# Mean squares per token from rows of x on ScalarE, and the norm factor spread by four products of 32 rows

## The chip, the cores and the metric

One core of a Trainium2 chip runs the kernel. The metric is the device time of one execution in microseconds. The time before is the median of three runs.

## What is computed

One inference layer of a hybrid decoder, for a prompt of 1024 tokens and 8 sequences of 4 new tokens: 1056 tokens of width 1024, all in f32. What matters here is the root mean square norm ahead of the combined projection:

```
y = x32 * lax.rsqrt(jnp.mean(x32 * x32, axis=-1, keepdims=True) + NORM_EPS)
h = y * norm_g
proj = jnp.einsum('btd,de->bte', h, w_in)        # 1024 -> 4608
qa, ka, va, ga, xb, gb, qc, kc, vc, gc = jnp.split(proj, SPLIT_IDX, axis=-1)
y = x + jnp.einsum('bte,ed->btd', mixed, w_out)  # mixed: retention, RG-LRU, window attention
```

The factor rsqrt(mean square + eps) is one number for each token. It commutes with the projection, so it can be applied to the projection's results.

## The kernel before

x lies transposed in memory (`x_T`): the 1024 features in 8 blocks of 128 partitions, the tokens along the free axis in three chunks of 352 (`xs`). Each f32 product is made of three passes over high and low parts (`h_hi`, `h_lo`, and `w_part` for the weights; lines 409 to 411). The 4608 output columns are 18 units of 256. Unit 0 comes first (`first_unit`). Units `qk`, `gB`, `xb`, `gC`, `gA` have 6 groups of 352 tokens; units `v`, `kvC` and `qC` have 9 groups with tokens on the partitions, 256 columns wide. A group is 24 products, in two halves; after half s of unit u every engine runs its `side(u, s)`, which places the smaller work by hand. Groups of units from 1 on use three banks of PSUM in turn (`proj_bank`), so group g waits until group g - 3 was read (`freed`). All engines run in program order; TensorE, ScalarE (`act`), VectorE (`dve`), GpSimd (`pool`) and SP, on whose queue nearly all transfers stand, meet by semaphores. Retention, RG-LRU, attention and at last the product with `w_out` follow, all interleaved with the projection's units on TensorE.

The norm's factor is made in units 1 and 2. ScalarE squares `xs` in six pieces of 4 x 352 columns (`x_square`, L820, at `SQUARE_AT` in unit 1), VectorE adds the eight feature blocks to one, `sqs` (`square_sum`, L1157 to L1163), and TensorE adds over the partitions with nine products against a column of ones at (1, 10) (`token_squares`, L451). VectorE divides and adds eps (`token_scale`), GpSimd takes the power -0.5 (L1638), so `rcol` has the factor with tokens on the partitions, nine columns. Where tokens lie along the free axis, the factor must stand in all partitions: VectorE multiplies nine identity tiles by `rcol` (`scale_diagonals`, L1180), TensorE multiplies ones (128 x 128) by each diagonal at (2, 3) (`spread_scale`, L461), and ScalarE copies the three banks to `rb` at (2, 4) (`spread_copy`, L827). ScalarE's evacuations of unit 2 use `rcol`; `rb` is read first by GpSimd and VectorE behind it.

The loads of weights (`load_w`, one unit of 1 MB into `raw`) wait until both engines have made the parts of the unit before.

Of the kernel before, what the change touches and what calls it, by code (L numbers as in the profile page):

```python
# [21 lines left out]
ALU = mybir.AluOpType  # L22
# [3 lines left out]
P = 128  # L26
# [75 lines left out]
def layer(nc, io):  # L102
    gammas = [float(1.0 - 2.0 ** (-5.0 - h)) for h in range(H)]
    with ExitStack() as ctx:
# [66 lines left out]
        with ExitStack() as r:  # L171

            sb("mixed_s", [P, 3 * H, TOK], scope=r)
            sb("under_v", [P, 2 * (NT + 1) * UNIT + N_CR], scope=r)
            sqt = sb("sqt", [P, 4 * CH], scope=r)
            sqs = sb("sqs", [P, TOK], scope=r)
            dgs = sb("dgs", [P, TOK], scope=r)
        with ExitStack() as r:
# [22 lines left out]
        with ExitStack() as r:  # L201
# [12 lines left out]

        names = """par_in ident_in const_in cr_in wg_in cc_in raw_in s0_in kcache_in vcache_in
            w0_in0 w0_in1 w0_in2 w0_in3 x_in0 x_in1 x_in2 x_in3 x_in4 x_in5 x_in6 x_in7 x_in8 x_in9 x_in10 x_in11
            x_again0 x_again1 x_again2 wo_in0 wo_in1 wo_in2 wo_in3
            stored_cache stored_ret stored_tails stored_kv stored_y0 stored_y1 stored_y2
            ones_set h_hi_set h_lo_set hs_set sq_set sq_added ms_done e9_set rcol_set ecol_set diag_set spread rb_set
            row_set gate_set ga_set ga_silu w_hi_set w_lo_set proj_done act_freed fold_set folded  # L220
# [22 lines left out]

        block = ctx.enter_context(nc.Block())

        def tile_rows(t):
# [12 lines left out]
        def _(sp):  # L259
# [26 lines left out]
            for c in range(1, 3):  # L286
# [3 lines left out]
            load_w(1)  # L290
            sp.dma_start(ident[:], io["c_ident"]).then_inc(S_["ident_in"], 16)
            sp.dma_start(gain[:].rearrange("p a d -> p (a d)"), io["qk_gain"].partition_broadcast(P)).then_inc(
                S_["const_in"], 16)
            sp.dma_start(st_T[:].rearrange("p f n -> p (f n)"), io["state_T"]).then_inc(S_["const_in"], 16)
            sp.dma_start(cr[:], io["c_ret"]).then_inc(S_["cr_in"], 16)

            for hd in range(H):
                if hd > 0:
                    sp.wait_ge(S_["stored_ret"], 32 * hd)
                else:  # L300
                    load_w(2)
                    load_w(3)
                    sp.wait_ge(S_["rb_set"], 3)
                sp.dma_start(s0[:], io["state_ret"][:, hd].rearrange("b d e -> d b e")).then_inc(S_["s0_in"], 16)
# [97 lines left out]
        WARM = 11  # L402
        SQUARE_AT = {0: (0, 0), 1: (0, 1), 2: (1, 0), 4: (1, 1), 6: (2, 0), 8: (2, 1)}

        @block.tensor
        def _(pe):
# [318 lines left out]
            def side(u, s):  # L725
                if u in RET_UNIT and s < 12:
# [7 lines left out]
                    if s < 9:  # L734
                        ret_one(base + s)
                if (u, s) == (1, 10):
                    token_squares()
                if (u, s) == (2, 3):
# [59 lines left out]
        def _(act):  # L798
# [17 lines left out]

            def x_square(c, half):
                if c + half > 0:
                    act.wait_ge(S_["sq_added"], 2 * c + half)
                act.activation(sqt[:].rearrange("p (k n) -> p k n", k=4), xs[c][:, 4 * half:4 * half + 4, :],  # L820
                               ACT.Square).then_inc(S_["sq_set"], 1)

            def spread_copy():
                for i in range(3):
                    n = 4 * P if i < 2 else NS
                    act.wait_ge(S_["spread"], i + 1)
                    act.activation(rb[:, i * 4 * P:i * 4 * P + n], bb[2 + i][:, 0:n], ACT.Copy).then_inc(  # L827
                        S_["rb_set"], 1)

# [301 lines left out]
        def _(dve):  # L1131
# [20 lines left out]

            def square_sum(c, half):

                total = sqs[:, c * CH:(c + 1) * CH]
                dve.wait_ge(S_["sq_set"], 2 * c + half + 1)
                link(dve.tensor_tensor(sqt[:, 0:2 * CH], sqt[:, 0:2 * CH], sqt[:, 2 * CH:4 * CH], ALU.add))  # L1157
                if half == 0:
                    dve.tensor_tensor(total, sqt[:, 0:CH], sqt[:, CH:2 * CH], ALU.add).then_inc(S_["sq_added"], 1)
                    return  # L1160
                link(dve.tensor_tensor(sqt[:, 0:CH], sqt[:, 0:CH], sqt[:, CH:2 * CH], ALU.add))
                dve.wait_ge(S_["sq_added"], 2 * c + 1)
                dve.tensor_tensor(total, total, sqt[:, 0:CH], ALU.add).then_inc(S_["sq_added"], 1)  # L1163

            def token_scale():

                link(dve.memset(ecol, 1.0))
                dve.wait_ge(S_["ms_done"], 1)
                pairs = bb[4][:, 0:2 * NT + 2].rearrange("p (t two) -> p t two", two=2)
                dve.tensor_scalar(ecol[:, 0:NT], pairs[:, 0:NT, 0], 1.0 / D, EPS, ALU.mult, ALU.add).then_inc(  # L1170
                    S_["e9_set"], 1)
                dve.tensor_scalar(ecol[0:NS, NT:NT + 1], pairs[0:NS, NT, 0:1], 1.0 / D, EPS, ALU.mult,
                                  ALU.add).then_inc(S_["e9_set"], 1)

            def scale_diagonals():
                dve.wait_ge(S_["ident_in"], 16)
                dve.wait_ge(S_["rcol_set"], 3)
                for t in range(NT + 1):
                    n = tile_rows(t)
                    dve.tensor_scalar(dgs[:, t * P:t * P + n], ident[:, 0:n], rcol[:, t:t + 1], None,  # L1180
                                      ALU.mult).then_inc(S_["diag_set"], 1)
                dve.tensor_scalar(ecol, ecol, EPS, None, ALU.mult).then_inc(S_["ecol_set"], 1)

            def sample_eps():
                dve.wait_ge(S_["rb_set"], 3)
# [28 lines left out]
            def ga_row(u, j):  # L1214
                g = FIRST_GROUP[u] + j
                dve.wait_ge(S_["proj_done"], g + 1)
                if (u, j) == (16, 0):
                    dve.wait_ge(S_["rb_set"], 3)
# [266 lines left out]
            def side(u, s):  # L1485
                if s - 1 in w_at(u) and u + 1 < NU:
                    w_low(u + 1, w_at(u).index(s - 1))
                if u in RET_UNIT and s < 12:
# [7 lines left out]
                    if s >= 3:  # L1496
                        ret_mix(base + s - 3)
                if u == 1 and s in SQUARE_AT:
                    square_sum(*SQUARE_AT[s])
                if (u, s) == (1, 10):  # L1500
# [75 lines left out]
        def _(pool):  # L1576
# [14 lines left out]
            def ret_qdec(m):  # L1591
# [3 lines left out]
                if m == 0:  # L1595
                    pool.wait_ge(S_["cr_in"], 16)
                    pool.wait_ge(S_["rb_set"], 3)
                    link(pool.memset(v_sel[NS:2 * NS], 0.0))
# [63 lines left out]
def constants():  # L1662
# [24 lines left out]
    for half in range(2):  # L1687
        for r, (b, g, s) in enumerate(rows):
# [5 lines left out]
            cc[r, C_BIASS + half * AKEYS:C_BIASS + (half + 1) * AKEYS] = row  # L1694
    return {"c_ident": np.eye(P, dtype=np.float32), "c_ret": cr.astype(np.float32), "c_att": cc.astype(np.float32)}


def laid_out(x):
# [31 lines left out]
    for a, name in enumerate(("w_rgate", "w_igate")):  # L1730
# [5 lines left out]
    state = np.concatenate([f["state_conv"].reshape(DB * 3, GW), f["state_lru"].reshape(DB, GW)])  # L1736
    return {
        "x_T": x.reshape(3, CH, KD, P).transpose(0, 3, 2, 1).reshape(3, P, KD * CH),
        "state_T": state.reshape(NS, H, P).transpose(2, 1, 0).reshape(P, H * NS),
# [30 lines left out]
```

## Time and profile before

| | us |
|---|---|
| median of three runs | 701.74 (701.61 to 701.86) |
| the profiled execution, its own time | 701.76 |
| its span, first to last instruction | 700.0 |
| TensorE busy | 692.3 |
| VectorE, ScalarE, GpSimd busy | 303.2, 263.0, 106.1 |

The span is what the profile covers; the time of an execution holds 1.76 us more around it. TensorE's granted clock was 1.00 throughout, its upper level of 2.4 GHz. An f32 product shows as two records; records overlap on TensorE, so their pitch (start to start) says more than their duration.

### The profile page before, as it was taken

The numbers are of one execution on the slowest core, as the hardware profiler recorded it, in microseconds if no ns is written. First come the engines' busy times: TensorE is split into PE (matmuls) and PEld (weight loads), VectorE is DVE, ScalarE is ACT, GpSimd is POOL, SyncE is SP. The second block draws the span as 40 slices with busy tenths as digits, with TensorE's granted clock in tenths as the row PEclk, the third lists the DMA queues.
The fourth block names the chain that finished last, engine by engine and source line by source line (L and its number), as shares of the span: only waits on it lengthen the run. The fifth ranks groups of instructions, "written<-read, shape, count | busy, mean of one in ns | idle before, by whom it ended". The sixth has DMA issues, their size and how long they took to land.

```text
span 700.0 us, 11867 instructions
## 1 busy us (share of the span) xinstructions
PE 692.3 (99%) x4688; PEld 671.7 (96%) x4688; DVE 303.2 (43%) x668; ACT 263.0 (38%) x642; POOL 106.1 (15%) x231
## 2 busy tenths in 40 slices
PE   8999999999999999999999999999999999999998
PEld 8999998999999999999999999899999999999998
DVE  6462452343434448875433374317533672500000
ACT  7562242322323343756616555325543460200000
POOL 0002171435354000000002222122100000000000
DMA  8402105122120311011041010131001351522221
GB/s 301 183 0 92 61 1 194 48 65 61 51 75 7 119 61 60 7 56 61 1 145 66 11 61 1 49 97 62 1 1 61 119 183 32 166 71 64 65 66 37
DMA packets 26803, 50.07 MB, mean 72 GB/s; under 512 B 2232, under 2 KB 20152, under 8 KB 24540
## 3 DMA queue, kind: packets, MB, share of 16 engines
q1 hardware_dynamic: 26748, 49.31, 21.4%
q8 instruction: 38, 0.62, 0.4%
q14 instruction: 17, 0.14, 0.1%
HBM read 42.22 MB, written 9.12 MB: 73 GB/s over the span
## 4 chain that ended last, share of the span: by engine, by line
PE 96%; DMA 1%; DVE 1%; issue 1%; ACT 1%; POOL 0%; SPq 0%; DVEq 0%; ACTq 0%
PE proj L409 22%; PE proj L411 22%; PE proj L410 22%; PE branch L411 4%; PE branch L410 4%; PE branch L409 4%; PE branch L589 2%; PE branch L654 2%; PE branch L631 2%; PE branch L505 1%; PE branch L522 1%; PE branch L537 1%; PE branch L543 1%; PE branch L644 1%; PE branch L525 1%; DMA mixed<-x_T 1%
## 5 line engine op out<-in xcount | busy, mean ns | idle before, releaser
L409 PE MATMUL proj<-big 128*128 128x352 f32 (+1 forms) x952 | 305.8, 321 | 1.6 <-DVE big L1148 1.2
L411 PE MATMUL proj<-big 128*128 128x352 f32 (+1 forms) x952 | 290.8, 305 | 0.0
L410 PE MATMUL proj<-big 128*128 128x352 f32 (+1 forms) x952 | 290.8, 305 | 0.0
L409 PEld LDWEIGHTS proj<-big 128*128 128x128 f32 x952 | 179.3, 188 | 5.4 <-ACT big L814 2.0
L410 PEld LDWEIGHTS proj<-big 128*128 128x128 f32 x952 | 179.4, 188 | 2.6 <-issue 1.9
L411 PEld LDWEIGHTS proj<-big 128*128 128x128 f32 x952 | 179.3, 188 | 0.0
L1143 DVE TENSOR_TENSOR big<-raw,big 128x512 fp32r<-128x512 f32 x72 | 48.8, 689 | 39.3 <-ACT big L808 39.3
L1588 POOL TENSOR_SCALAR stat<-stat 128x1 f32<-128x1 f32 (+2 forms) x68 | 18.0, 264 | 278.7 <-ACT junk L934 189.5
L411 PE MATMUL branch<-m_hi,big 128*128 128x352 f32 x180 | 58.0, 322 | 0.0
L410 PE MATMUL branch<-m_lo,big 128*128 128x352 f32 x180 | 58.0, 322 | 0.0
L409 PE MATMUL branch<-m_hi,big 128*128 128x352 f32 x180 | 57.9, 322 | 0.0
L808 ACT ACTIVATE big<-raw 128x512 fp32r<-128x512 f32 x72 | 44.0, 625 | 3.4 <-DMA par<-params 2.6
L1589 POOL TENSOR_TENSOR stat<-stat 128x1 f32<-128x1 f32 (+2 forms) x68 | 40.1, 589 | 5.7
L1241 DVE SCALAR_TENSOR_TENSOR sT<-branch,stat,cr 128x128 f32<-128x128 f32 (+1 forms) x36 | 12.2, 338 | 58.4 <-PE branch L505 54.4
L411 PE MATMUL proj<-m_hi,big 128*128 128x352 f32 x108 | 34.8, 322 | 0.0
L410 PE MATMUL proj<-m_lo,big 128*128 128x352 f32 x108 | 34.8, 322 | 0.0
L409 PE MATMUL proj<-m_hi,big 128*128 128x352 f32 x108 | 34.7, 322 | 0.0
L1571 DVE TENSOR_TENSOR xy<-branch,xy 128x352 f32<-128x352 f32 x15 | 7.9, 524 | 61.8 <-PE branch L411 61.8
L409 PEld LDWEIGHTS branch<-m_hi,big 128*128 128x128 f32 x180 | 33.8, 188 | 0.0
L411 PEld LDWEIGHTS branch<-m_hi,big 128*128 128x128 f32 x180 | 33.8, 188 | 0.0
L410 PEld LDWEIGHTS branch<-m_lo,big 128*128 128x128 f32 x180 | 33.8, 188 | 0.0
L1379 DVE SCALAR_TENSOR_TENSOR kn<-proj,stat,gain 128x128 f32<-128x128 f32 (+1 forms) x18 | 6.3, 349 | 50.3 <-POOL stat L1589 50.3
(219 smaller groups left out, 964.5 us busy)
## 6 DMA issues: line engine op xcount, KB each, us to landing
raw<-w_units SPq DMA_DIRECT2D x17, 1024.0 KB, 4.9
mixed<-x_T SPq DMA_DIRECT2D x12, 352.0 KB, 7.9
xy<-x_T SPq DMA_DIRECT2D x24, 176.0 KB, 2.4
out_y_T<-xy SPq DMA_DIRECT2D x24, 176.0 KB, 1.9
raw<-w_out SPq DMA_DIRECT2D x6, 512.0 KB, 4.5
xy<-w_out SPq DMA_DIRECT2D x6, 512.0 KB, 4.2
s<-state_ret SPq DMA_DIRECT2D x4, 512.0 KB, 3.9
out_s_ret<-s SPq DMA_DIRECT2D x4, 512.0 KB, 3.2
```

The lines of the kernel that those rows point to most:

```text
L409: pe.matmul(out, a_lo, b_hi, start=first, stop=False)
L410: pe.matmul(out, a_hi, b_lo, start=False, stop=False)
L411: return pe.matmul(out, a_hi, b_hi, start=False, stop=last)
L589: pe.matmul(bb[GATE_BANKS[q]][:, 0:CH], wg[:, gate, f, :], cv[:, f % 2, c * CH:(c + 1) * CH], start=True, stop=True).then_inc(S_["gates_do ...
L631: mm = pe.matmul(bb[1][:, g * 2 * P + lo:(g + 1) * 2 * P], qT[:, (9 * half + t) % 2, g * P:(g + 1) * P], kT[:, half, (t - 1) * P + lo:(t + ...
L654: mm = pe.matmul(bb[3][:, 0:2 * P], v_c[:, half, t - 1 + kt, :], pT[:, n8 % 2, kt * 2 * P:(kt + 1) * 2 * P], start=(kt == 0 or t == 0), st ...
L808: act.activation(w_part(u % 2, 0)[:, cols], raw[:, cols], ACT.Copy).then_inc(S_["w_hi_set"], 1)
L1143: dve.tensor_tensor(w_part(u % 2, 1)[:, cols], raw[:, cols], w_part(u % 2, 0)[:, cols].bitcast(F32), ALU.subtract).then_inc(S_["w_lo_set"], 1)
L1241: dve.scalar_tensor_tensor(out=sT[0:n, m % 2, 0:n], in0=bb[0][0:n, 0:n], scalar=rcol[0:n, c:c + 1], in1=mask, op0=ALU.mult, op1=ALU.mult). ...
L1571: dve.tensor_tensor(y_out[:, g % 3, :], y_banks[f][:, 0:CH], x_res[:, g % 3, :], ALU.add).then_inc(S_["y_set"], 1)
L1588: link(pool.tensor_scalar(ss, ss, 1.0 / DH, ecol[0:n, t:t + 1], ALU.mult, ALU.add))
L1589: return pool.tensor_tensor(rs, ss, neghalf[0:n, 0:w], ALU.pow)
```

## The change

The mean squares are taken from x by rows. `x_prompt` and `x_sample` are inputs of their own, loaded in nine tiles of 128 tokens x 1024 (the last has 32 tokens), three into new space (`xt`) and six over the parts of `xs` that VectorE has finished with (SP waits for `h_lo_set`). ScalarE squares each tile in place with an accumulated sum over the row, at s = 0 to 8 of unit 1, and the sum lands where `token_scale` reads it. `square_sum` and `token_squares` are gone.

The diagonal is folded: `dgs` has for each token tile 32 columns in place of 128; row p of tile t holds the factor of token p at column p mod 32. Four products with 32 rows each (32r to 32r + 31) of ones and of `dgs` spread the factor of the tokens 32r to 32r + 31 of all eight tiles into a bank each, 256 columns; a fifth does the 32 sample tokens. ScalarE copies them to `rb` with an output that steps by 128. SP also loads `ident_32`, four identities of 32 x 32 one above the other.

```
             for t in range(NT + 1):                      # SP, behind the load of cr
                 if t >= 3:
                     sp.wait_ge(S_["h_lo_set"], KD * ((t - 3) // 2 + 1))
                 src = io["x_prompt"][t * P:(t + 1) * P, :] if t < NT else io["x_sample"]
                 sp.dma_start(x_tok[t][0:tile_rows(t), :], src).then_inc(S_[f"xt_in{t}"], 16)
...
-            def token_squares():
-                pe.wait_ge(S_["ones_set"], 1)
-                pe.wait_ge(S_["sq_added"], 6)
-                for t in range(NT + 1):
-                    mm = pe.matmul(bb[4][0:tile_rows(t), 2 * t:2 * t + 2], sqs[:, chunk_cols(t)], ones[:, 0:2],
-                                   start=True, stop=True)
-                mm.then_inc(S_["ms_done"], 1)
-
             def spread_scale():
-                for t in range(NT + 1):
-                    if t % 4 == 0:
-                        pe.wait_ge(S_["diag_set"], min(t + 4, NT + 1))
-                    n = tile_rows(t)
-                    mm = pe.matmul(bb[(2, 3, 4)[t // 4]][:, (t % 4) * P:(t % 4) * P + n], ones[:],
-                                   dgs[:, t * P:t * P + n], start=True, stop=True)
-                    if t % 4 == 3 or t == NT:
-                        mm.then_inc(S_["spread"], 1)
+                pe.wait_ge(S_["diag_set"], 1)
+                for r in range(4):
+                    rows = slice(32 * r, 32 * r + 32)
+                    pe.matmul(bb[1 + r][:, 0:32 * NT], ones[rows, :], dgs[rows, 0:NT, :].rearrange("p t n -> p (t n)"),
+                              start=True, stop=True).then_inc(S_["spread"], 1)
+                pe.matmul(bb[0][:, 0:NS], ones[0:32, :], dgs[0:32, NT, :], start=True,
+                          stop=True).then_inc(S_["spread"], 1)
...
-            def x_square(c, half):
-                if c + half > 0:
-                    act.wait_ge(S_["sq_added"], 2 * c + half)
-                act.activation(sqt[:].rearrange("p (k n) -> p k n", k=4), xs[c][:, 4 * half:4 * half + 4, :],
-                               ACT.Square).then_inc(S_["sq_set"], 1)
+            def x_square(t):
+                act.wait_ge(S_[f"xt_in{t}"], 16)
+                x = x_tok[t][0:tile_rows(t), :]
+                act.activation(x, x, ACT.Square, accum_out=row_ss[0:tile_rows(t), t:t + 1]).then_inc(S_["sq_set"], 1)
...
                 dve.wait_ge(S_["rcol_set"], 3)
-                for t in range(NT + 1):
-                    n = tile_rows(t)
-                    dve.tensor_scalar(dgs[:, t * P:t * P + n], ident[:, 0:n], rcol[:, t:t + 1], None,
-                                      ALU.mult).then_inc(S_["diag_set"], 1)
+                dve.tensor_tensor(dgs[:], ident_32[:, None, :].to_broadcast((P, NT + 1, 32)),
+                                  rcol.unsqueeze(2).to_broadcast((P, NT + 1, 32)), ALU.mult).then_inc(S_["diag_set"], 1)
...
-                if u == 1 and s in SQUARE_AT:
-                    x_square(*SQUARE_AT[s])
+                if u == 1 and s <= NT:
+                    x_square(s)
```

On TensorE, at (1, 10), these rows of before stand between two projection products; nothing stands in their place now. `branch` is a bank of PSUM, `sqs` the sums over feature blocks.

```order
278 L411 MATMUL proj<-big 128x352
279 L451 MATMUL branch<-ones,sqs 128x2 [waits sq_added,ones_set]
280 L451 MATMUL branch<-ones,sqs 128x2 x7
281 L451 MATMUL branch<-ones,sqs 32x2
282 L409 MATMUL proj<-big 128x352
```

So the nine products and their wait for VectorE are gone. On TensorE at (2, 3), the spread before:

```order
341 L411 MATMUL proj<-big 128x256
342 L461 MATMUL branch<-dgs,ones 128x128 [waits diag_set]
343 L461 MATMUL branch<-dgs,ones 128x128 x3
344 L461 MATMUL branch<-dgs,ones 128x128 [waits diag_set]
345 L461 MATMUL branch<-dgs,ones 128x128 x3
346 L461 MATMUL branch<-dgs,ones 128x32 [waits diag_set]
347 L409 MATMUL proj<-big 128x256 [waits act_freed]
```

And at the same place now (lines 417 to 419 of the changed kernel are 409 to 411 of before):

```order
338 L419 MATMUL proj<-big 128x256
339 L460 MATMUL branch<-dgs,ones 128x256 [waits diag_set]
340 L460 MATMUL branch<-dgs,ones 128x256 x3
341 L462 MATMUL branch<-dgs,ones 128x32
342 L417 MATMUL proj<-big 128x256 [waits act_freed]
```

Nine products became five, four of them twice as wide, and there is one wait. On ScalarE in unit 1, the squares and evacuations before:

```order
36 L820 ACTIVATE sqt<-mixed 128x1408
37 L868 ACTIVATE mixed<-proj 128x352 [waits proj_done]
38 L820 ACTIVATE sqt<-mixed 128x1408 [waits sq_added] x2
39 L868 ACTIVATE mixed<-proj 128x352 [waits proj_done]
40 L808 ACTIVATE big<-raw 128x512 [waits proj_done,raw_in]
41 L820 ACTIVATE sqt<-mixed 128x1408 [waits sq_added]
42 L868 ACTIVATE mixed<-proj 128x352 [waits proj_done]
```

And now (867 is 868, 805 is 808; `xt` and `mixed` hold rows of x):

```order
36 L817 ACTIVATE xt,sp_t<-xt 128x1024 [waits xt_in0]
37 L867 ACTIVATE mixed<-proj 128x352 [waits proj_done]
38 L817 ACTIVATE xt,sp_t<-xt 128x1024 [waits xt_in1]
39 L817 ACTIVATE xt,sp_t<-xt 128x1024 [waits xt_in2]
40 L867 ACTIVATE mixed<-proj 128x352 [waits proj_done]
41 L805 ACTIVATE big<-raw 128x512 [waits proj_done,raw_in]
42 L817 ACTIVATE mixed,sp_t<-mixed 128x1024 [waits xt_in3]
43 L817 ACTIVATE mixed,sp_t<-mixed 128x1024 [waits xt_in4]
44 L867 ACTIVATE mixed<-proj 128x352 [waits proj_done]
```

Two squares stand ahead of each evacuation, and they wait for transfers in place of VectorE.

## Rows read from the trace of the kernel before

**Rows 1.** The page: busy time by engine; chain that ended last, by engine.
```profile
PE 692.3 (99%) x4688; PEld 671.7 (96%) x4688; DVE 303.2 (43%) x668; ACT 263.0 (38%) x642; POOL 106.1 (15%) x231
...
PE 96%; DMA 1%; DVE 1%; issue 1%; ACT 1%; POOL 0%; SPq 0%; DVEq 0%; ACTq 0%
```

**Rows 2.** TensorE's waits, whole span: who was waited for; us, times, longest.
```profile
PE proj L409 <- DVE big L1148: 1.2, 1, 1.2
PE branch L426 <- POOL ones L1634: 1.1, 1, 1.1
PE branch L644 <- ACT pT L987: 0.8, 2, 0.6
```

**Rows 3.** TensorE's timeline around L451: start us, us from first start to end.
```profile
51.91 0.33 PE L411 MATMUL proj<-big 128*128 128x352 f32 x1
52.07 2.00 PE L451 MATMUL branch<-ones,sqs 128*128 128x2 f32 x18
53.99 0.43 PE L409 MATMUL proj<-big 128*128 128x352 f32 x1
54.26 0.32 PE L410 MATMUL proj<-big 128*128 128x352 f32 x1
```

**Rows 4.** TensorE's timeline around L461.
```profile
61.59 0.27 PE L411 MATMUL proj<-big 128*128 128x256 f32 x1
61.71 2.09 PE L461 MATMUL branch<-dgs,ones 128*128 128x128 f32 x18
63.63 0.36 PE L409 MATMUL proj<-big 128*128 128x256 f32 x1
63.83 0.28 PE L410 MATMUL proj<-big 128*128 128x256 f32 x1
```

**Rows 5.** TensorE's timeline in attention, a product of 256 columns.
```profile
441.82 1.02 PE L654 MATMUL branch<-pT,v_c 128*128 128x256 f32 x4
442.68 0.27 PE L684 MATMUL branch<-ident,kcT 128*64 128x128 f32 x1
```

**Rows 6.** TensorE's timeline in attention, a product of 32 rows.
```profile
454.03 0.27 PE L411 MATMUL proj<-big 128*128 128x256 f32 x1
454.24 0.43 PE L699 MATMUL branch<-kcT,v_c 32*128 32x64 f32 x2
454.60 0.28 PE L702 MATMUL branch<-kcT,cache 128*128 128x8 f32 x1
```

**Rows 7.** ScalarE's timeline, 40 to 67 us (idle before, releaser).
```profile
40.53 0.62 ACT L808 ACTIVATE big<-raw 128x512 fp32r<-128x512 f32 x1
...
50.36 0.47 ACT L868 ACTIVATE mixed<-proj 128x352 f32<-128x352 f32 x1 [0.81 <-PE proj L411]
...
66.79 0.47 ACT L863 ACTIVATE v_tok<-proj,stat 128x256 f32<-128x256 f32 x1 [2.41 <-PE proj L411]
```

**Rows 8.** ScalarE's groups of instructions, shapes apart: xcount | busy us, mean ns.
```profile
L882 ACT ACTIVATION_READ_ACCUMULATOR o_sq<-branch 128x1 f32 x32 | 6.4, 199 | 0.0
...
L916 ACT ACTIVATE rg<-aa 128x1056 f32<-128x1056 f32 x4 | 4.4, 1088 | 0.1
```

**Rows 9.** Busy time in three stretches of 10 us.
```profile
core 0: us, PE busy (x) PEld busy (x) DVE busy (x) ACT busy (x) POOL busy (x), PEclk, DMA share, GB/s
10.00:20.00 10.00, 10.00 (x63) 10.00 (x64) 9.46 (x19) 9.78 (x22) 0.00 (x0) 1.00 1.04 411
20.00:30.00 10.00, 10.00 (x65) 10.00 (x64) 4.64 (x9) 4.32 (x9) 0.00 (x0) 1.00 0.61 212
30.00:40.00 10.00, 10.00 (x65) 10.00 (x64) 3.36 (x5) 5.02 (x6) 0.00 (x0) 1.00 0.01 2
```

**Rows 10.** Timelines of SP's queue, VectorE and GpSimd.
```profile
24.99 27.61 SPq L268 DMA_DIRECT2D raw<-w_units  x2
...
18.09 4.06 DVE L1148 SCALAR_TENSOR_TENSOR big<-mixed,par,big 128x352 fp32r<-128x352 f32 x8 [0.42 <-ACT big L814]
...
54.48 2.52 POOL L1638 TENSOR_TENSOR stat<-stat 128x4 f32<-128x4 f32 x3 [53.38 <-DVE stat L1172]
```

More of the change, by code:

```diff
@@ L174, in layer @@
             sb("under_v", [P, 2 * (NT + 1) * UNIT + N_CR], scope=r)
-            sqt = sb("sqt", [P, 4 * CH], scope=r)
-            sqs = sb("sqs", [P, TOK], scope=r)
-            dgs = sb("dgs", [P, TOK], scope=r)
+            xt = sb("xt", [P, 3, D], scope=r)
+            dgs = sb("dgs", [P, NT + 1, 32], scope=r)
+            ident_32 = sb("ident_32", [P, 32], scope=r)
         with ExitStack() as r:
@@ L212, in layer @@
         wo_raw = [raw[:, 0:D], raw[:, D:2 * D], stage[:, 0:D], stage[:, D:2 * D]]
-        names = """par_in ident_in const_in cr_in wg_in cc_in raw_in s0_in kcache_in vcache_in
+        names = """par_in ident_in ident_32_in const_in cr_in wg_in cc_in raw_in s0_in kcache_in vcache_in
             w0_in0 w0_in1 w0_in2 w0_in3 x_in0 x_in1 x_in2 x_in3 x_in4 x_in5 x_in6 x_in7 x_in8 x_in9 x_in10 x_in11
-            x_again0 x_again1 x_again2 wo_in0 wo_in1 wo_in2 wo_in3
+            xt_in0 xt_in1 xt_in2 xt_in3 xt_in4 xt_in5 xt_in6 xt_in7 xt_in8 x_again0 x_again1 x_again2 wo_in0 wo_in1 wo_in2 wo_in3
             stored_cache stored_ret stored_tails stored_kv stored_y0 stored_y1 stored_y2
-            ones_set h_hi_set h_lo_set hs_set sq_set sq_added ms_done e9_set rcol_set ecol_set diag_set spread rb_set
+            ones_set h_hi_set h_lo_set hs_set sq_set e9_set rcol_set ecol_set diag_set spread rb_set
             row_set gate_set ga_set ga_silu w_hi_set w_lo_set proj_done act_freed fold_set folded
@@ L244, in layer @@
         block = ctx.enter_context(nc.Block())
+        x_tok = [*(xt[:, t, :] for t in range(3)),
+                 *(flat[:, c * KD * CH + i * D:c * KD * CH + (i + 1) * D] for c in range(3) for i in range(2))]
+        row_ss = sp_t[:].rearrange("p a h -> p (a h)")[:, 8:17]
         def tile_rows(t):
@@ L291, in _ @@
             sp.dma_start(ident[:], io["c_ident"]).then_inc(S_["ident_in"], 16)
+            sp.dma_start(ident_32[:], io["c_ident_32"]).then_inc(S_["ident_32_in"], 16)
             sp.dma_start(gain[:].rearrange("p a d -> p (a d)"), io["qk_gain"].partition_broadcast(P)).then_inc(
@@ L295, in _ @@
             sp.dma_start(cr[:], io["c_ret"]).then_inc(S_["cr_in"], 16)
+            for t in range(NT + 1):
+                if t >= 3:
+                    sp.wait_ge(S_["h_lo_set"], KD * ((t - 3) // 2 + 1))
+                src = io["x_prompt"][t * P:(t + 1) * P, :] if t < NT else io["x_sample"]
+                sp.dma_start(x_tok[t][0:tile_rows(t), :], src).then_inc(S_[f"xt_in{t}"], 16)
             for hd in range(H):
@@ L302, in _ @@
                     load_w(3)
-                    sp.wait_ge(S_["rb_set"], 3)
+                    sp.wait_ge(S_["rb_set"], 5)
                 sp.dma_start(s0[:], io["state_ret"][:, hd].rearrange("b d e -> d b e")).then_inc(S_["s0_in"], 16)
@@ L402, in layer @@
         WARM = 11
-        SQUARE_AT = {0: (0, 0), 1: (0, 1), 2: (1, 0), 4: (1, 1), 6: (2, 0), 8: (2, 1)}
         @block.tensor
@@ L815, in x_hi @@
                                scale=par[:, PAR["norm_g"] + k:PAR["norm_g"] + k + 1]).then_inc(S_["h_hi_set"], 1)
-            def x_square(c, half):
-                if c + half > 0:
-                    act.wait_ge(S_["sq_added"], 2 * c + half)
-                act.activation(sqt[:].rearrange("p (k n) -> p k n", k=4), xs[c][:, 4 * half:4 * half + 4, :],
-                               ACT.Square).then_inc(S_["sq_set"], 1)
-            def spread_copy():
[L824 to L828, printed above, removed]
+            def x_square(t):
+                act.wait_ge(S_[f"xt_in{t}"], 16)
+                x = x_tok[t][0:tile_rows(t), :]
+                act.activation(x, x, ACT.Square, accum_out=row_ss[0:tile_rows(t), t:t + 1]).then_inc(S_["sq_set"], 1)
+            def spread_copy():
+                for r in range(5):
+                    act.wait_ge(S_["spread"], r + 1)
+                    if r < 4:
+                        act.activation(rb[:, 0:SEQ].rearrange("p (t r n) -> p r t n", t=NT, r=4)[:, r],
+                                       bb[1 + r][:, 0:32 * NT].rearrange("p (t n) -> p t n", t=NT),
+                                       ACT.Copy).then_inc(S_["rb_set"], 1)
+                    else:
+                        act.activation(rb[:, SEQ:TOK], bb[0][:, 0:NS], ACT.Copy).then_inc(S_["rb_set"], 1)
             def gate_silu(r):
@@ L1151, in x_lo @@
                                          op1=ALU.subtract).then_inc(S_["h_lo_set"], 1)
[L1153 to L1163, printed above, removed]
@@ L1165, in token_scale @@
             def token_scale():
                 link(dve.memset(ecol, 1.0))
-                dve.wait_ge(S_["ms_done"], 1)
-                pairs = bb[4][:, 0:2 * NT + 2].rearrange("p (t two) -> p t two", two=2)
-                dve.tensor_scalar(ecol[:, 0:NT], pairs[:, 0:NT, 0], 1.0 / D, EPS, ALU.mult, ALU.add).then_inc(
+                dve.wait_ge(S_["sq_set"], NT + 1)
+                dve.tensor_scalar(ecol[:, 0:NT], row_ss[:, 0:NT], 1.0 / D, EPS, ALU.mult, ALU.add).then_inc(
                     S_["e9_set"], 1)
-                dve.tensor_scalar(ecol[0:NS, NT:NT + 1], pairs[0:NS, NT, 0:1], 1.0 / D, EPS, ALU.mult,
+                dve.tensor_scalar(ecol[0:NS, NT:NT + 1], row_ss[0:NS, NT:NT + 1], 1.0 / D, EPS, ALU.mult,
@@ L1182, in scale_diagonals @@
                 dve.tensor_scalar(ecol, ecol, EPS, None, ALU.mult).then_inc(S_["ecol_set"], 1)
             def sample_eps():
-                dve.wait_ge(S_["rb_set"], 3)
+                dve.wait_ge(S_["rb_set"], 5)
                 rs = rb[:, SEQ:TOK]
@@ L1217, in ga_row @@
                 if (u, j) == (16, 0):
-                    dve.wait_ge(S_["rb_set"], 3)
+                    dve.wait_ge(S_["rb_set"], 5)
                 bank = proj_bank(g)
@@ L1497, in side @@
                         ret_mix(base + s - 3)
-                if u == 1 and s in SQUARE_AT:
-                    square_sum(*SQUARE_AT[s])
                 if (u, s) == (1, 10):
@@ L1596, in ret_qdec @@
                     pool.wait_ge(S_["cr_in"], 16)
-                    pool.wait_ge(S_["rb_set"], 3)
+                    pool.wait_ge(S_["rb_set"], 5)
                     link(pool.memset(v_sel[NS:2 * NS], 0.0))
@@ L1694, in constants @@
             cc[r, C_BIASS + half * AKEYS:C_BIASS + (half + 1) * AKEYS] = row
-    return {"c_ident": np.eye(P, dtype=np.float32), "c_ret": cr.astype(np.float32), "c_att": cc.astype(np.float32)}
+    return {"c_ident": np.eye(P, dtype=np.float32), "c_ident_32": np.tile(np.eye(32, dtype=np.float32), (4, 1)),
+            "c_ret": cr.astype(np.float32), "c_att": cc.astype(np.float32)}
 def laid_out(x):
@@ L1737, in laid_out @@
     return {
+        "x_prompt": f["x_prompt"].reshape(SEQ, D), "x_sample": f["x_sample"].reshape(NS, D),
         "x_T": x.reshape(3, CH, KD, P).transpose(0, 3, 2, 1).reshape(3, P, KD * CH),
```

4 lines of the change are left out of this document (1 added, 3 removed).

## The prediction

> **What bounds the kernel now.** I read the page's busy shares first, then the chain that ended last, then TensorE's list of waits over the whole span, and only then single stretches. The busy shares [rows 1] give TensorE 692.3 of 700.0 us, and the chain that ended last is TensorE for 96% of the span. TensorE's waits [rows 2] come to 4.4 us in all (six lines, from 1.2 down to 0.3; the three longest are shown), at the start, at the first projection products, at one transpose of retention and in attention. None lies in units 1 and 2, where this change works: TensorE is busy 10.00 us in every stretch of 10 from 10 to 70 (six rows alike, three shown in [rows 9]). So in this stretch a product that is taken out of TensorE's queue is worth the time by which it pushes its successors back. Work on VectorE, ScalarE, GpSimd or the queues is worth nothing unless it makes TensorE wait. The reader should read every edit with that question: does it shorten TensorE's queue, or make that queue wait?
>
> **The change, part by part.**
>
> *Token squares taken off TensorE.* The nine products of two columns (L451) show as 18 records, two for each f32 product [rows 3]. How far they push the queue is read from starts, not from durations, since records overlap: from the L411 at 51.91 to the L410 at 54.26 is 2.35 us; without anything between, these are two steps of 0.16 (as 51.91 to 52.07), 0.32. The block costs 2.35 - 0.32 = **2.03 us**, all of it on the path, and nothing takes its place on TensorE.
>
> *The spread, before.* By the same reading [rows 4], from L411 at 61.59 to L410 at 63.83 is 2.24 us, against two steps of 0.12 = 0.24: **2.00 us** for nine products, 18 records of at most 128 columns.
>
> *The spread, after: serial cost.* Four products of 256 columns and one of 32, each again two records. The nearest row for 256 f32 columns is L654 in attention [rows 5]: four records from 441.82 to the next start at 442.68, 0.215 us each. Eight such are 1.72 us. The small one: two records at the pitch of the small f32 records (18 in 53.99 - 52.07 = 1.92, so 0.107 each), 0.21 us. The queue's first projection product after an f32 block is followed by its neighbour 0.20 instead of 0.12 us later [rows 4]: 0.08 more. And a product on 32 rows costs something by itself: in [rows 6] L411 at 454.03, two records of L699 (32 rows), then L702 (128 rows) at 454.60. That is 0.57 us, less 0.12 for L411 and 0.21 for two small full-height records: **0.24 us** for going to 32 rows and back. Serial sum: 1.72 + 0.21 + 0.08 + 0.24 = 2.25 us, 0.25 more than before.
>
> *The spread, after: can the four overlap?* They read four different strips of 32 rows of `ones` and `dgs` and write four different banks, so they share only the queue. The trace of before has no products on different strips side by side, so it shows neither answer. I bound it. Serial: 2.25. All four at once: two passes of 0.215 and the rest, 0.43 + 0.21 + 0.08 + 0.24 = 0.96. In between: the two passes of one product use the same strip and the same bank, so they follow each other, but the second pass of one can run beside the first pass of the next if starts stay in program order. That gives five steps of 0.215 for the four = 1.08, and the first record of the small one beside the last big pass, 0.11: 1.08 + 0.11 + 0.08 + 0.24 = **1.51 us**. I take this middle value: it needs only that different strips don't block each other, and no reordering. Against before it gives back 0.49 us; the ends give -0.25 (a loss) and 1.04.
> The Trainium skill ("TensorEngine Tiling (Array Packing)", Key Properties) says that tiles on different strips work in parallel and that a change of tiling mode drains TensorE. The second half agrees with the 0.24 us of [rows 6]. No row of before shows the first half. The Trainium skill's page "TensorE: Matmul & The Clock Gate" (Measured speedup vs the span model) gives 3.07 times for four strips of 512 columns; by that the 1.72 would be 0.56 us, an estimate from that page, near my lower end.
>
> *ScalarE.* Six squares of 1408 columns become nine of 1024. A 1056-column Square takes 1.09 us and reading an accumulator 0.20 [rows 8]: 1.06 + 0.20 = 1.26 each, 11.3 us. I lay them into the timeline of before [rows 7]. Evacuations of unit 1 already wait for TensorE (0.81 us ahead of the one at 50.36). The slots hold two squares (2.5), one evacuation (0.45) and one weight piece (0.62) per group, 3.6 us against a group of 24 products of 0.16 = 3.84 us. So ScalarE just keeps pace: the evacuation at 50.36 stays there. Even if it fell behind, three banks rotate, so an evacuation may be two groups, 7.7 us, late before TensorE waits. Cost 0; cover 7.7 us.
>
> *Loads.* x by rows is 8 x 512 KB + 128 KB = 4.3 MB, put into SP's queue behind cr and ahead of the load of unit 2 (24.99) [rows 10]. Three go out at once; the waits on h_lo_set of the others end when VectorE's chunks do, the last at 22.2 us (18.09 + 4.06), before 24.99. So SP is not held. The DMA engines move 411 GB/s in 10:20 and are at 0.01 in 30:40 [rows 9]. If nothing of x went before 22.2, at that rate it would be in at 22.2 + 10.4 = 32.6 and unit 2's weights (1 MB, 2.6 us, next in the queue) at 35.2. ScalarE first wants those at 40.53 [rows 7]. At the 212 GB/s of 20:30 it would be 42.5 and 47.5: the weights 7.0 late, still inside the 7.7 us of the banks. Unit 1's weights and the first x blocks stand ahead of all this. Cost 0. The small load of ident_32 is one more issue and hides there too.
>
> *VectorE, GpSimd, the copies.* Fifteen additions and eight of nine diagonal products go. Now the factor chain starts at the last square (about 50 us) instead of behind L451, then GpSimd's powers, 2.52 us [rows 10]. The diagonals would be ready near 56, before the spread at about 59.7. It was not a wait of TensorE before [rows 2], so this gains nothing. Five copies to rb instead of three, in shorter pieces; even at twice the time of before they would stay under the 2.41 us that ScalarE idles ahead of the next evacuation, waiting for TensorE [rows 7]. Cost 0.
>
> **Sum.** 2.03 + 0.49 = 2.52 us less. The profiled execution took 701.76 us (1.76 around the span of 700.0), 0.02 over the median of the runs, so nothing is to be corrected: 701.76 - 2.5 = **699.2 us**.
>
> **The rivals.**
> 1. *Strips run one after another* (27%). For it: no row shows an overlap, and starts are in program order. Against: nothing shared. 2.03 - 0.25 = 1.78 less: 700.0.
> 2. *All four strips at once* (11%). It needs a later product's first pass to overtake an earlier one's second. 2.03 + 1.04 = 3.07 less: 698.7. This is where the rule of the Trainium skill's "TensorE: Matmul & The Clock Gate" quoted above would bring it.
> 3. *Every change of strip drains like the change of height* (7%). The 0.24 of [rows 6] is then paid five times, 0.96 more than serial: 1.78 - 0.96 = 0.82 less: 700.9, no measurable change. For it: only that the one price I have is not split into its causes.
> 4. *The squares arrive late and TensorE waits for a bank* (3%); the one that ends slower. ScalarE stands at a square in front of an evacuation in unit 1. From the last square's slot (near 49 us) the loads may be 7.7 us late; from 56.7 us on each us is lost, and from 59.2 on the gain is gone. At 62 us it would be 2.8 slower: 704.5. That needs 4.3 MB to take 40 us from 22 on, about 108 GB/s, against 411 and 212 measured and empty engines in 30:40.
> 5. *The token squares are worth less than their push* (2%): a wait later on, such as the 0.8 us in attention, grows by what is saved. Against: the waits behind unit 2 are on chains that TensorE itself feeds. Some 701.2.
> The forecast itself (strips overlap by pairs) has 50%.
>
> **How the numbers follow.** What this kernel's measurement can tell from no change is 0.2%, 1.4 us, so "faster" is below 700.3. The forecast and rivals 1 and 2 are all faster: 88%. Rivals 3 and 5 are the same: 9%. Rival 4: 3%. The range reaches from the full overlap (698.7) to serial (700.0), with some 0.4 us for a start whose first waits hang on a transfer [rows 2], and a part of rival 3: 698.3 to 700.5.
>
> **What the profile will show.** Right: no L451 group; TensorE's records fall by 18 and 8, from 4688 to 4662; the L410 behind the fifth spread product starts 1.5 + 0.24 us after the L411 ahead; the first record of the last big product starts some 0.65 us after that of the first, not 1.3 as in series; no waits of TensorE for ScalarE in units 1 and 2; the square's read of x lands before its slot. The step on strips is wrong if the eight big records span 1.7 us or 0.45. The whole is wrong if a PE wait for `proj` released by ScalarE appears in 30 to 60 us, or if a late wait in attention has grown by some 2 us.

## The result and the profile after

The changed kernel takes 698.5 us (median of five runs, 698.28 to 698.75) against 701.74 of the kernel before on the same chip. The ratio is 0.995, with an interval of 0.9939 to 0.9962. On a second chip the same program took 698.38 (five runs) against 701.72 (nine): 0.9954, 0.9941 to 0.9967. The changed kernel is faster by 3.2 to 3.3 us, and 2.5 were forecast. The median lies inside the range; the gain is 0.7 to 0.8 us larger than forecast, and one step of the sum is the main reason.

The page of the changed kernel, busy time by engine and the chain that ended last, as [rows 1]:

```profile
span 696.8 us, 11812 instructions
...
PE 688.7 (99%) x4662; PEld 667.9 (96%) x4662; DVE 291.9 (42%) x645; ACT 264.6 (38%) x656; POOL 106.1 (15%) x231
...
PE 95%; ACT 1%; DVE 1%; DMA 1%; issue 1%; POOL 0%; SPq 0%; DVEq 0%
```

TensorE has 26 records fewer, as counted ahead, and is busy 3.6 us less. ScalarE is busy 1.6 us more, VectorE 11.3 less, and neither of the two shows in the span: what counts is TensorE's queue. Its list of waits, as [rows 2]:

```profile
PE proj L417 <- DVE big L1147: 1.9, 2, 1.1
PE branch L434 <- POOL ones L1616: 1.1, 1, 1.1
PE branch L643 <- ACT pT L986: 0.8, 2, 0.6
```

The third line is that of before; no wait in attention has grown. The first belongs to the first projection products, before 10 us, and is not the change's (it returns below). TensorE's timeline around the spread, as [rows 4]:

```profile
59.51 0.27 PE L419 MATMUL proj<-big 128*128 128x256 f32 x1
59.72 0.71 PE L460 MATMUL branch<-dgs,ones 32*128 32x256 f32 x8
60.25 0.30 PE L462 MATMUL branch<-dgs,ones 32*128 32x32 f32 x2
60.48 0.39 PE L417 MATMUL proj<-big 128*128 128x256 f32 x1
60.70 0.28 PE L418 MATMUL proj<-big 128*128 128x256 f32 x1
```

Read as before: 60.70 - 59.51 = 1.19, less two steps of 0.12, is **0.95 us** for the block. Before it was 2.00. The eight big records take 0.53 us from their first start to the next block's. That is no more than the first two records of a single strip need (with one strip, e3 below, the third record starts 0.54 us after the first). The view of line L460, cut once to 59.70:59.74 and once to 59.70:60.30 (durations in ns, minimum, median, maximum), tells how many start together:

```profile
L460 PE MATMUL branch<-dgs,ones x4: 478/478/478, 59.7 to 59.7; 32*128 32x256 f32 x4
...
L460 PE MATMUL branch<-dgs,ones x8: 374/426/478, 59.7 to 60.1; 32*128 32x256 f32 x8
```

Four records start within 0.02 us from 59.72 on and the other four from 60.0 on. No record names its strip. Since records of one strip start at least 0.21 us apart (e3), the four that start together are on four strips: the first passes of all four products run side by side, then the second passes. ScalarE's timeline in unit 1, as [rows 7] (row 40.53 of before is 39.26 here, 50.36 is 50.31):

```profile
38.86 0.46 ACT L867 ACTIVATE mixed<-proj 128x352 f32<-128x352 f32 x1 [1.28 <-PE proj L419]
39.26 0.63 ACT L805 ACTIVATE big<-raw 128x512 fp32r<-128x512 f32 x1
39.80 1.04 ACT L817 ACTIVATE mixed<-mixed 128x1024 f32<-128x1024 f32 x1
40.75 0.18 ACT L817 ACTIVATION_READ_ACCUMULATOR mixed<-mixed 128x1 f32 x1
40.84 1.04 ACT L817 ACTIVATE mixed<-mixed 128x1024 f32<-128x1024 f32 x1
...
50.31 0.47 ACT L867 ACTIVATE mixed<-proj 128x352 f32<-128x352 f32 x1 [0.76 <-PE proj L419]
```

Every evacuation of unit 1 waits for TensorE, none of the squares waits for a transfer, and a square with its accumulator costs 1.04 us from start to start (39.80 to 40.84), not 1.26. In the kernel before this was not so for every evacuation, as the prediction had read it from the one at 50.36. Those at 40.19, 43.09 and 46.55 waited for nothing but the square ahead of them, and that square had waited for VectorE:

```profile
38.91 1.38 ACT L820 ACTIVATE sqt<-mixed 128x1408 f32<-128x1408 f32 x1 [2.08 <-DVE sqs L1163]
40.19 0.45 ACT L868 ACTIVATE mixed<-proj 128x352 f32<-128x352 f32 x1
```

So the change gave ScalarE room in unit 1, which the time does not show, since TensorE waited for no evacuation before either. The stretches of 10 us, as [rows 9], show the loads:

```profile
20.00:30.00 10.00, 10.00 (x64) 10.00 (x64) 4.33 (x8) 3.99 (x9) 0.00 (x0) 1.00 1.03 396
30.00:40.00 10.00, 10.00 (x65) 10.00 (x64) 0.07 (x1) 5.64 (x12) 0.00 (x0) 1.00 0.70 249
```

The added 4.3 MB fill what was free there, at 396 and 249 GB/s, under a TensorE that stays busy 10.00 of 10.

### The profile page after: what moved, and what is told of

Its sections match the earlier page's. It is cut to its first block, busy times and chain, and to the rows that moved or that the text cites. A ratio compares the mean times of both kernels' runs of the same rounds, so it can differ in the third digit from the quotient of the medians.

```text
span 696.8 us, 11812 instructions
## 1 busy us (share of the span) xinstructions
PE 688.7 (99%) x4662; PEld 667.9 (96%) x4662; DVE 291.9 (42%) x645; ACT 264.6 (38%) x656; POOL 106.1 (15%) x231
## 4 chain that ended last, share of the span: by engine, by line
PE 95%; ACT 1%; DVE 1%; DMA 1%; issue 1%; POOL 0%; SPq 0%; DVEq 0%
PE proj L417 22%; PE proj L419 21%; PE proj L418 21%; PE branch L419 4%; PE branch L418 4%; PE branch L417 4%; PE branch L588 2%; PE branch L653 2%; PE branch L630 2%; PE branch L504 1%; PE branch L521 1%; PE branch L536 1%; PE branch L542 1%; PE branch L643 1%; PE branch L524 1%; DMA mixed<-x_T 1%
## 5 line engine op out<-in xcount | busy, mean ns | idle before, releaser
L886 ACT ACTIVATE o_nrm<-branch,stat 128x128 f32<-128x128 f32 x32 | 11.8, 368 | 41.7 <-DVE mixed L1266 33.4
```

The source lines that it names most:

```text
L886: act.activation(o_nrm[:, m % 2, :], bb[1 + m % 2][:, 0:P], ACT.Copy, scale=stat[:, 8 + m % 2:9 + m % 2]).then_inc(S_["o_set"], 1)
```

## The experiments

Twelve experiments ran. Several of their kernels differ by one us of 700, and the time of a run spreads by as much, so the block is read from the trace of each: from the start of the projection record ahead of it to the second behind it, less two steps of 0.12. The block repeats to the hundredth between runs.

**e1, token squares alone.** The changed kernel with the spread of before:

```
-                for r in range(4):
-                    ...
+                for t in range(NT + 1):
+                    mm = pe.matmul(bb[(2, 3, 4)[t // 4]][:, (t % 4) * P:(t % 4) * P + n], ones[:],
+                                   dgs[:, t * P:t * P + n], start=True, stop=True)
```

> The token squares alone: rows of x on ScalarE, no products of token squares, but the spread as before (nine products of 128 rows). Theory A (each part is worth its push on TensorE's queue): 2.03 us less than before, 699.7, and the spread block again 2.00 us. Rival (part of the gain comes from elsewhere, the first waits or VectorE's freed time): less than 1.5 or more than 2.6 us.

700.16 us against 701.69, 0.9985 (0.9977 to 0.9994): 1.5 us by the medians, the interval 0.4 to 1.6 where 2.03 was expected. The block is 60.84 to 63.08, again 2.00 us. The profiled execution took 701.4 and shows what the times hide, in the first records of the projection,

```profile
7.76 0.63 PE L415 MATMUL proj<-big 128*128 128x352 f32 x1 [2.41 <-DVE big L1143]
8.19 0.49 PE L416 MATMUL proj<-big 128*128 128x352 f32 x1
8.48 0.49 PE L417 MATMUL proj<-big 128*128 128x352 f32 x1
```

and, by stretches of 1 us with the granted clock third from the end:

```profile
8.00:9.00 1.00, 1.00 (x4) 1.00 (x5) 0.85 (x2) 0.75 (x3) 0.00 (x0) 0.50 0.89 305
9.00:10.00 1.00, 1.00 (x5) 1.00 (x5) 0.92 (x2) 1.00 (x3) 0.00 (x0) 0.50 1.00 375
```

TensorE had waited 2.41 us for its first operands, and then the granted clock stood at 0.50, its lower level of 1.2 GHz, until about 11 us: a pitch of 0.29 us in place of 0.16. The eleven times form two clusters, seven from 699.8 to 700.3 and four from 701.2 to 701.7. The times differ from execution to execution by 1.9 us, nearly as much as the 2.03 us in question. Taking the start away settles it. The first record of unit 1's second group stands at the same place in all queues. In the kernel before, in the changed one and here:

```profile
34.90 0.32 PE L409 MATMUL proj<-big 128*128 128x352 f32 x1
...
34.85 0.32 PE L417 MATMUL proj<-big 128*128 128x352 f32 x1
...
36.17 0.32 PE L415 MATMUL proj<-big 128*128 128x352 f32 x1
```

From there to the record ahead of the spread it is 61.59 - 34.90 = 26.69 us before, 59.51 - 34.85 = 24.66 in the changed kernel and 60.84 - 36.17 = 24.67 here: 2.02 to 2.03 us less, in both kernels that lack the token squares. And what follows the record ahead of the spread, less the block, is 700.0 - 61.59 - 2.00 = 636.4 us in the kernel before, 636.3 in the changed one, and in the ten experiments other than e7 and e9 from 636.3 to 636.7 (636.7 here, where the extra 0.3 lies behind TensorE's last product). So the rest of TensorE's queue does not answer to the change, and the rival's "elsewhere" doesn't exist behind the block. The 2.03 us of the token squares are shown by the trace. The times confirm only that this kernel is faster: even its faster cluster lies 1.4 to 1.9 us under the median of the kernel before, and one profiled execution can't say where the rest went in the others.

**e2, the spread alone.** The kernel before, with the folded diagonal, five products and five copies:

```
                 def token_squares(): ...        # as before, nine products
-                dve.tensor_scalar(dgs[:, t * P:t * P + n], ident[:, 0:n], rcol[:, t:t + 1], ...)    # x9
+                dve.tensor_tensor(dgs[:], ident_32 ..., rcol ..., ALU.mult)
```

> The spread alone: folded diagonal and four strips, token squares by sums over feature blocks as before. If the four strips run all at once, the spread block costs 0.95 us in place of 2.00 and the kernel 1.05 less than before, 700.7. If the block is short only because of what stood ahead of it (rows of x, an idle VectorE), it is 1.5 us or more here.

700.6 against 701.69: 1.1 us less, 0.999 (0.9981 to 0.9999). The two blocks:

```profile
51.90 2.00 PE L453 MATMUL branch<-ones,sqs 128*128 128x2 f32 x18
...
61.42 0.27 PE L413 MATMUL proj<-big 128*128 128x256 f32 x1
61.62 0.71 PE L462 MATMUL branch<-dgs,ones 32*128 32x256 f32 x8
62.16 0.30 PE L464 MATMUL branch<-dgs,ones 32*128 32x32 f32 x2
62.39 0.39 PE L411 MATMUL proj<-big 128*128 128x256 f32 x1
62.61 0.28 PE L412 MATMUL proj<-big 128*128 128x256 f32 x1
```

62.61 - 61.42 - 0.24 = 0.95 us, with the token squares standing ahead at their old price. The overlap is the strips' own.

**e3, all four on one strip.**

```
-                    rows = slice(32 * r, 32 * r + 32)
+                    rows = slice(0, 32)
```

> The changed kernel with all four wide products of the spread on the same strip, rows 0 to 31 of ones and of the diagonals, still into four banks, so three quarters of the factors are wrong. If different strips are what lets them overlap, they now run in series: the block costs my serial sum, 2.25 us, 1.3 more than the 0.95 of the changed kernel. If small height alone or different banks let them overlap, it stays at 0.95.

```profile
58.67 0.27 PE L419 MATMUL proj<-big 128*128 128x256 f32 x1
58.88 1.99 PE L460 MATMUL branch<-dgs,ones 32*128 32x256 f32 x8
60.71 0.30 PE L462 MATMUL branch<-dgs,ones 32*128 32x32 f32 x2
60.94 0.39 PE L417 MATMUL proj<-big 128*128 128x256 f32 x1
61.16 0.28 PE L418 MATMUL proj<-big 128*128 128x256 f32 x1
```

2.25 us, the serial sum to the hundredth (by two misses that cancel, see e4). Same height, same banks, same columns: only the strips differ, so they are what gives the overlap. The eight records take 1.83 us against 0.53 to 0.54 for eight on four strips, a factor of 3.4. They start 0.216 us apart but for the first step after the change of height, which takes 0.32; the mean is 0.229. (Its one time, 699.09, is 0.6 above the changed kernel's median, not 1.3: it had the earliest start of all, the record ahead of the block at 58.67 against 59.51.)

**e4, full height.** The five products on all 128 rows:

```
-                    rows = slice(32 * r, 32 * r + 32)
+                    rows = slice(0, P)
```

> The changed kernel with the five products of the spread over all 128 rows instead of 32, same columns and banks (the factors are sums over four strips, so wrong). If going to 32 rows and back costs 0.24 us, the block costs 1.72 + 0.21 + 0.08 = 2.01 us, 0.24 less than with one strip of 32. If the price of 32 rows was something else in that attention row (a wait, the columns), it costs the same as one strip.

61.64 - 59.46 - 0.24 = 1.94 us (2.01 expected). The eight big records take 1.72 us as summed, the small product 0.14 and not 0.21:

```profile
59.57 1.89 PE L460 MATMUL branch<-dgs,ones 128*128 128x256 f32 x8
61.29 0.30 PE L462 MATMUL branch<-dgs,ones 128*128 128x32 f32 x2
61.43 0.36 PE L417 MATMUL proj<-big 128*128 128x256 f32 x1
```

Against e3's 2.25, going to 32 rows and back costs 0.31 us; [rows 6] had given 0.24. So the serial sum was 0.07 too high in one term and 0.07 too low in another, and its agreement with e3 is luck. So the strips pay an entry of 0.31 and earn 1.30. Four products of 256 columns in place of eight of 128 are alone worth 0.06 (2.00 to 1.94).

**e5 and e6, two strips in two orders.**

```
-                    rows = slice(32 * r, 32 * r + 32)
+                    rows = slice(32 * (r // 2), 32 * (r // 2) + 32)      # e5: 0, 0, 1, 1
+                    rows = slice(32 * (r % 2), 32 * (r % 2) + 32)        # e6: 0, 1, 0, 1
```

> The changed kernel with the four wide products on two strips in the order 0, 0, 1, 1 (half of the factors wrong). One wave of passes costs 0.46 us (a strip's two records, 0.229 each in the run with one strip), and the block of the changed kernel, one wave, 0.95. Theory O (starts in program order, a product waits only for its own strip): the third starts with the second, so three waves, 1.87 us. Theory R (products of a free strip go ahead of ones that wait): two waves, 1.41 us. All in series would be 2.25.

> The same with the order 0, 1, 0, 1 (half of the factors wrong). Both theories: two waves, 1.41 us. If it is 1.87 or more, two products on different strips do not run fully side by side when others of the same strip follow.

e5: 60.90 - 59.27 - 0.24 = 1.39 us. e6: 61.05 - 59.43 - 0.24 = 1.38 us. The view of line L460 in e5, cut to 59.45:59.60 and to 59.45:59.90:

```profile
L460 PE MATMUL branch<-dgs,ones x2: 478/478/478, 59.5 to 59.5; 32*128 32x256 f32 x2
...
L460 PE MATMUL branch<-dgs,ones x4: 374/426/478, 59.5 to 59.8; 32*128 32x256 f32 x4
```

Already the first two records start together, though the second product of the program is on the same strip as the first. On one strip (e3) the second record starts 0.32 us after the first, so the record beside it must be of the other strip: the third product went ahead of the second. This is inferred, since no record names its product. The time of the block says the same: theory R (1.41) holds and O (1.87) falls. Between these two orders there is no difference; the number of products on the fullest strip counts, and each more on it costs 0.43 us (0.95, 1.38 and, for four, 2.25).

**e7, the strips apart.** The five products in five successive halves of groups:

```
-                if (u, s) == (2, 3):
-                    spread_scale()
+                if u == 2 and 3 <= s < 8:
+                    spread_scale(s - 3)
```

> The changed kernel with the five products of the spread issued in five successive halves, from (2, 3) to (2, 7), with projection products of 128 rows between. Each then pays its own 0.46 (0.23 for the small one), the 0.31 us of going to 32 rows and back, and 0.08 behind it: about 4 x 0.46 + 0.23 + 5 x 0.39 = 4.0 us in all, 3.1 more than the block of the changed kernel. If the 0.31 is not paid for each change of height, it is near 2.3 + 0.4 = 2.7.

The first of them:

```profile
59.24 0.27 PE L419 MATMUL proj<-big 128*128 128x256 f32 x1
59.44 0.69 PE L460 MATMUL branch<-dgs,ones 32*128 32x256 f32 x2
60.06 0.39 PE L417 MATMUL proj<-big 128*128 128x256 f32 x1
60.29 0.28 PE L418 MATMUL proj<-big 128*128 128x256 f32 x1
```

60.29 - 59.24 - 0.24 = 0.81 us; the next three 0.82, 0.82, 0.81, the small one 0.52: 3.78 in all against 0.95 together. The one run took 701.26 us. Each change of height is paid. A change of strip alone is not (that was rival 3), or the changed kernel's block of 0.95 us would have no room for it.

**e8 and e9, late rows.** The loads of the last two tiles wait for TensorE, and the next weights go ahead of them:

```
             for t in range(NT + 1):
+                if t == 7:
+                    load_w(2)
+                    sp.wait_ge(S_["proj_done"], 10)      # e9: 11
```

> The changed kernel with the loads of the last two row tiles held until TensorE has ended group 9 (about 46.4 us); the load of unit 2's weights goes ahead of them, so only the last two squares are late. They land near 49 and the last square ends near 51.2, 1.7 later than in the changed kernel. My written cover (7.7 us, the banks) and the shorter one I now read (2.8 us: behind the last square stand an evacuation 0.46, the last weight piece 0.62 and VectorE's low part 0.69, and unit 2 starts at 53.9) both say: TensorE does not wait in units 1 and 2, no change.

> The same, held until group 10 has ended (about 50.2 us): the last square ends near 55.0, 5.5 us later than in the changed kernel. By the cover of 7.7 us nothing changes. By the cover of 2.8 us TensorE waits for VectorE's low part at the start of unit 2, some 2.7 us, and the kernel is as much slower.

In e8 the transfer landed later than thought, and the last square ended at 52.6 (49.5 in the changed kernel), 3.1 us late. The first product of unit 2 starts 0.37 behind its forerunner instead of 0.16, a wait of 0.2 us where none was expected: the cover is just used up. e9, ScalarE and then TensorE:

```profile
53.92 1.06 ACT L819 ACTIVATE mixed<-mixed 128x1024 f32<-128x1024 f32 x1 [6.40 <-DMA mixed<-x_prompt]
...
53.81 0.32 PE L421 MATMUL proj<-big 128*128 128x352 f32 x1
57.75 0.45 PE L419 MATMUL proj<-big 128*128 128x256 f32 x1 [3.62 <-DVE big L1144]
57.99 0.42 PE L420 MATMUL proj<-big 128*128 128x256 f32 x1
```

The last square ended at 56.1, 6.6 us late, and TensorE stood still 3.8 us (57.75 - 53.81 - 0.16). So the cover is 2.8 us, not the 7.7 us of the banks: behind the last square stand the last weight piece on ScalarE and its low part on VectorE, and unit 2 needs them. Behind the gap the clock stood at 0.50 until 61.2, a pitch of 0.21 for 0.12, 1.5 us more. 704.08 us in all (one run), slower than the kernel before. Late squares do make TensorE wait, as rival 4 said, but for a weight piece and not for a bank, and much sooner than I wrote.

**e10, e11 and e12: again, four products, a longer warm-up.** e10 is the changed kernel, the partner of the two others, which both beat the kernel before as it does.

```
                 for r in range(4):                       # e11 and e12
+                    tiles = NT + 1 if r == 0 else NT     # the 32 sample tokens ride in strip 0
...
-        WARM = 11                                        # e12
+        WARM = 14
```

> The changed kernel once more, as the partner of the next ones on the same chip: 3.08 us less than the kernel before (2.03 for the token squares, 1.05 for the spread), with the spread of some tenths that the first waits and the clock of the start put on every run.

> The changed kernel with the fifth product folded into the first (288 columns of strip 0 instead of 256 and 32 apart). The block should cost 0.95 less the small product's two records (0.23), plus twice 32 columns more in one strip (0.05): 0.77, so 0.18 us less, seen in the block's starts and too little to be told apart by the time. If the small product was hidden beside the big ones, nothing is saved in the block.

> The kernel of four products with 14 instead of 11 warm-up products at the start, which shortens the idle stretch ahead of the first projection product by about 0.6 us. If the second cluster of times, 1.3 us above the first, comes from the clock falling to its lower level after that stretch (seen in the run with rows only), the cluster is gone and the median some tenths lower. If it comes from late transfers, both stay; should the warm-up run into the first projection, the time rises by up to 0.6.

e10: 698.38 us (698.05 to 700.15). e11: 698.69 (698.38 to 700.01), ratio to the kernel before 0.9955, 0.9941 to 0.9969. Its block is 62.03 - 60.93 - 0.24 = 0.86, 0.09 less, half of what was expected; where the other half went isn't shown. By the time it can't be told from e10. e12: 698.6 (698.13 to 698.71), 0.9952, 0.9939 to 0.9964, the same block. Its five times lie within 0.6 us; e10 and e11 have one each at 700.0 and above. The stretches of e10's profiled execution, its time 700.15 and its first wait 1.93 us, show the lower clock again:

```profile
9.00:10.00 1.00, 1.00 (x5) 1.00 (x4) 0.96 (x2) 0.85 (x2) 0.00 (x0) 0.50 0.99 351
10.00:11.00 1.00, 1.00 (x5) 1.00 (x5) 0.69 (x1) 0.72 (x3) 0.00 (x0) 0.50 1.03 407
```

In e12 the first wait was 0.8 us and the clock 1.00 throughout. Five runs are too few to say that the slower cluster is gone, and the median didn't move. No version is measurably better than the changed kernel.

## Why the prediction was wrong in its size

**Right.** TensorE's queue bounds the stretch, and only what leaves it counts: the part behind the block is the same in before and after to 0.1 us. Token squares 2.03 us: no record of them is left, nothing stands in their place. The spread before, 2.00. The serial sum, 2.25 against 2.25 in e3, but by luck: the price of 32 rows, 0.24 by [rows 6], measured 0.31, and the small product, 0.21, measured 0.14 at full height (e4). That price is paid once in the block and not for each strip. The loads and the squares: no wait of TensorE for either.

**The step that failed** is "I take this middle value: it needs only that different strips don't block each other, and no reordering". The middle 1.51 us was wrong, the block costs 0.95, which was my lower bound (0.96) and rival 2, held at 11%. The gain of the spread is 1.05 us where the sum had 0.49. I had argued that a later product's first pass would have to overtake an earlier one's second and took this for unlikely without a row on it; by the view of line L460 and by e5 it does so. My signs for this step had no place for what came: I had named 0.45 us and 1.7 us, and the eight big records took 0.53, with the first records of the first and the last big product 0.02 us apart where I had written 0.65. The Trainium skill's "TensorEngine Tiling (Array Packing)" (Key Properties), that tiles on different strips work in parallel, is borne out by e3 against the changed kernel, 2.25 against 0.95. The factor 3.07 of "TensorE: Matmul & The Clock Gate" in the Trainium skill (Measured speedup vs the span model) was the better guide too: 3.4 was measured here, on 256 f32 columns. With 0.95 in it, the sum is 2.03 + 1.05 = 3.08 and the forecast 698.7; the medians moved by 3.24 and, on the other chip, 3.34. The remaining 0.2 to 0.3 is within what the start does to a run (0.5 us among the five runs of the changed kernel alone). In the two profiled executions the account closes to 0.1: their spans differ by 3.2 us, of which 2.03 lie between unit 1's second group and the spread, 1.05 in the spread, 0.05 ahead of them and less than 0.1 behind.

That 698.5 lies inside the range of 698.3 to 700.5 is no merit of the middle value: the lower end had been set for the full overlap of rival 2 and an early start.

**Wrong without effect.** The evacuations of unit 1 before the change, three of which did not wait for TensorE. The square with its accumulator, 1.26 us for 1.04. And the cover of 7.7 us for late squares. I had asked which bank would be missed and not which weight piece stands behind the square on ScalarE; e8 and e9 give 2.8 us. Rival 4's sum, 704.5 us for loads ending at 62 us, is nearly reached (704.08, of which some 1.5 us by the clock) with the last loads landing near 54.

## What to carry to other kernels

Where TensorE is busy 99%, count the pushes in its queue first, and then ask what may make it wait. Four f32 products of 32 rows and 256 columns on four different strips and four banks, with a small fifth, cost 0.95 us, one such product alone 0.81 (e7). Going to that height and back costs 0.31 us each time: put them together. Whether it also holds with fewer banks wasn't tried. For a step that is moved to another engine, look for the cover in everything that stands behind it on that engine, weight pieces too, not only in the buffer that it frees.

## What the runs showed of the hardware

- Products seem to overtake others in TensorE's queue when their strip is free: with the order of strips 0, 0, 1, 1 the block took 1.39 us, with 0, 1, 0, 1 it took 1.38, and in both two records start together at once; all on one strip took 2.25.
- The start decides more than half a us of a run. The granted clock fell to 0.50 for some 3 us after first waits of 1.93, 1.98 and 2.41 us (e10, e11, e1) and after the gap of 3.8 us in e9; in the eleven other profiled executions, with first waits of 0.8 to 1.7 us, it stayed at 1.00 there. From the first projection product to unit 1's second group the three took 28.4 to 28.5 us, the others 26.9 to 28.0, short waits on the way included. A fall explains the slower cluster of e1 in part only: the mean clock was 0.998 in three of its four executions, but 1.00 in the one of 701.17 us.
- A Square of 1024 columns whose output goes over its own input took 1.05 us and the read of its accumulator 0.19; the next square started 1.04 us after the first, since the records overlap.
